# Expert rows fetched from and added to HBM by indirect transfers in a mixture-of-experts decoder trunk

## The reference

```python
def swiglu(h, w_gate_up, w_down):
    g, u = jnp.split(h @ w_gate_up, 2, axis=-1)
    return (jax.nn.silu(g) * u) @ w_down

def moe_ffn(h, router, w_gate_up, w_down):
    t = h.reshape(B * S, D)                       # 256 x 1024
    logits = (t @ router).astype(jnp.float32)     # 256 x 8
    top_v, top_i = lax.top_k(logits, TOP_K)
    gates = jax.nn.softmax(top_v, axis=-1)
    combine = jnp.sum(jax.nn.one_hot(top_i, N_EXPERTS) * gates[..., None], axis=1)
    out = jnp.zeros_like(t)
    for e in range(N_EXPERTS):                    # w_gate_up[e]: 1024 x 7168, w_down[e]: 3584 x 1024
        out = out + combine[:, e:e + 1] * swiglu(t, w_gate_up[e], w_down[e])
    return out
```

## Time and profile before

| | us |
|---|---|
| median of 3 runs | 1529.01 (1528.96 to 1530.62) |
| the profiled execution, its own time | 1530.43 |
| its span in the profile | 1528.6 |
| PE busy | 1487.6 (97%) |
| DVE busy | 1166.1 (76%) |
| ACT busy | 963.4 (63%) |
| POOL busy | 32.6 (2%) |
| bytes moved | 431.78 MB, 282 GB/s over the span |

### The profile page before, as it was taken

One profiled execution on the slowest core, in us unless ns is written; L12 is line 12 of the kernel. 1 busy time (PEld: TensorE's weight loads), 2 busy tenths in 40 slices (PEclk: granted clock), 3 DMA queues, 4 the chain that ended last, 5 costly groups with the idle time before them and its releaser, 6 DMA issues.

```text
span 1528.6 us, 20344 instructions
## 1 busy us (share of the span) xinstructions
PE 1487.6 (97%) x7137; PEld 1251.9 (82%) x7137; DVE 1166.1 (76%) x914; ACT 963.4 (63%) x838; POOL 32.6 (2%) x81
## 2 busy tenths in 40 slices
PE   7999999999989899999999999999999999999997
PEld 7997788888878778888888888888888888888885
DVE  4566545554674599899899899889989989989985
ACT  6454544444683387777677677677767667767764
POOL 1010000000020000000000000000000000000000
PEclk9999999999999899999999999999999999999999
DMA  8544455554353389999999999999999999999992
GB/s 284 192 138 143 160 185 185 181 191 158 91 190 111 110 326 381 329 377 363 339 363 366 337 356 380 357 328 377 358 323 378 368 335 363 360 342 359 380 354 83
DMA packets 207522, 431.78 MB, mean 282 GB/s; under 512 B 14261, under 2 KB 54650, under 8 KB 207482
## 3 DMA queue, kind: packets, MB, share of 16 engines
q1 hardware_dynamic: 207194, 430.20, 78.9%
q0 software_dynamic: 288, 1.05, 0.2%
HBM read 430.15 MB, written 1.05 MB: 282 GB/s over the span
## 4 chain that ended last, share of the span: by engine, by line
PE 95%; DVE 2%; ACT 2%; issue 1%; SPq 0%; DMA 0%; ACTq 0%; DVEq 0%
PE PS L1530 19%; PE PS L1534 19%; PE PS L1531 19%; PE PS L1241 5%; PE PS L1242 5%; PE PS L1243 5%; PE PS L1005 4%; PE PS L1490 2%; PE PS L1055 2%; PE PS L1050 2%; PE PS L1052 2%; PE PS L1501 1%; PE PS L1104 1%; PE PS L1107 1%; PE PS L1101 1%
## 5 line engine op out<-in xcount | busy, mean ns | idle before, releaser
L1681 DVE TENSOR_TENSOR wlo<-ring,whi 128x2048 fp32r<-128x2048 f32 x334 | 762.7, 2291 | 114.0 <-ACT whi L662 112.3
L662 ACT ACTIVATE whi<-ring 128x2048 fp32r<-128x2048 f32 x334 | 639.6, 1918 | 233.2 <-PE PS L1534 222.1
L1530 PE MATMUL PS<-whi,xhi 128*128 128x512 f32 x864 | 341.1, 395 | 0.4 <-ACT whi L662 0.4
L1531 PE MATMUL PS<-whi,xlo 128*128 128x512 f32 x864 | 336.8, 390 | 0.0
L1534 PE MATMUL PS<-wlo,xhi 128*128 128x512 f32 x864 | 231.4, 390 | 0.2 <-DVE wlo L1681 0.2
L1534 PEld LDWEIGHTS PS<-wlo,xhi 128*128 128x128 f32 x864 | 162.1, 188 | 34.7 <-DVE wlo L1681 0.6
L1530 PEld LDWEIGHTS PS<-whi,xhi 128*128 128x128 f32 x864 | 162.3, 188 | 33.2 <-ACT whi L662 0.7
L1531 PEld LDWEIGHTS PS<-whi,xlo 128*128 128x128 f32 x864 | 162.4, 188 | 32.5
L1530 PE MATMUL PS<-whi,hhi 128*128 128x512 f32 x440 | 172.7, 393 | 0.0
L1531 PE MATMUL PS<-whi,hlo 128*128 128x512 f32 x440 | 171.3, 389 | 0.0
L1647 DVE TENSOR_TENSOR wlo<-ring,whi 128x2048 fp32r<-128x2048 f32 x42 | 96.3, 2292 | 67.4 <-ACT whi L630 67.4
(11 more groups left out here) (333 smaller groups left out, 1650.4 us busy)
## 6 DMA issues: line engine op xcount, KB each, us to landing
ring<-in_moe_w_gate_up SPq DMA_DIRECT2D x448, 512.0 KB, 5.4
ring<-in_moe_w_down SPq DMA_DIRECT2D x224, 512.0 KB, 5.5
ring<-in_dense_w_gate_up SPq DMA_DIRECT2D x56, 512.0 KB, 4.6
ring<-in_dense_w_down SPq DMA_DIRECT2D x28, 512.0 KB, 4.2
ring<-in_a_w_in SPq DMA_DIRECT2D x12, 768.0 KB, 7.6
ring<-in_mem_w_kv SPq DMA_DIRECT2D x4, 1024.0 KB, 5.3
ring<-in_a_w_out SPq DMA_DIRECT2D x4, 1024.0 KB, 4.9
ring<-in_b_w_out SPq DMA_DIRECT2D x4, 1024.0 KB, 5.0
```

Source lines behind the costliest of these rows:

```text
L662: nc.scalar.activation(whi[:, j, :], ring[:, h * SLOT:(h + 1) * SLOT], ACT.Copy).then_inc(S("highs"), 1)
L1530: mm(out_, lhsT=xh, rhs=whi[:, j, c0:c0 + HD], start=first, stop=False)
L1531: mm(out_, lhsT=xl, rhs=whi[:, j, c0:c0 + HD], start=False, stop=False)
L1681: v.tensor_tensor(wlo[:, j, :], ring[:, h * SLOT:(h + 1) * SLOT], whi[:, j, :].bitcast(F32), ALU.subtract).then_inc(S("lows"), 1)
```

## The change

**Tokens to an expert.** The normalised tokens are stored once to a scratch tensor `xg` in HBM, and the residual stream once to the output itself. From expert 1 on, POOL fetches the rows of the next expert by an indirect transfer (`fetch_rows`) with a list of token numbers, one for each slot (`slot_tok`), into `xs` (the SBUF of `xn`), as rows. PE turns them with 8 transposes (`turn_rows`) at block 6. Expert 0 still uses `gather`.

**The list.** `slot_values` replaces `turn_gates`: two products of `Sx` with two columns `ct`, the gate and the token's number. It runs at block 3 and 5 of expert 0 and at block 5 of the others; DVE copies both columns. The keys are made otherwise: a token that isn't chosen gets a place behind the chosen ones, so that every one of the 256 keys of an expert is used and each of the 128 slots holds a different token, with gate 0 where the token wasn't chosen. That needs `counts` and more DVE steps.

**Results back.** In block 1 ACT writes gate times y as one f32 tile `ys` (`y_out`), and POOL adds its 128 rows to the output in HBM by an indirect transfer with addition (`put_rows`). `combine`, `y_low`, `G` and `add` are gone, and SP's final store too. After the last expert, ACT and DVE each do half of y, and POOL does the last `put_rows` and waits for all of them.

**Waits.** PE waits at block 6 for `rows_in` ahead of `turn_rows`. DVE waits at block 4 for the last scatter (`putting`, `scattered`) before it overwrites gate and list, and at block 5 for `slots_turned` and `fetching`. POOL's `pause` operations (one element each) order its transfers with DVE. Some semaphores are merged (`q_t` and `k_t` into `heads_t`, others alike), which changes no order; POOL's `iota` comes earlier.

```diff
+        xg_d = nc.dram_tensor("xg", [SEQ, D], F32)
+        xs, ys = xn[0:CAP, 0], xn[0:CAP, 1]
@@ sync
-            for t in range(NT):
-                sp.wait_ge(S("x_final"), t + 1)
-                sp.dma_start(out[0].rearrange("(t p) d -> p t d", p=P)[:, t], xres[:, t]).then_inc(S("stored"), 16)
-            sp.wait_ge(S("stored"), 16 * NT)
@@ gpsimd
+            pool.wait_ge(S("x_sum"), 9)
+            for t in range(NT):
+                pool.dma_start(out[0][t * P:(t + 1) * P], xres[:, t]).then_inc(S("stored"), 16)
+            pool.wait_ge(S("x3_gained"), 1)
+            for t in range(NT):
+                pool.dma_start(xg[t * P:(t + 1) * P], xn[:, t]).then_inc(S("xg_in"), 16)
+            pool.wait_ge(S("xg_in"), 16 * NT)
+            def fetch_rows(i):
+                pool.wait_ge(S("slots"), i + 1)
+                pool.tensor_tensor(pause, nhalf[0:1, 0:1], nhalf[0:1, 0:1], ALU.mult).then_inc(S("fetching"), 1)
+                pool.indirect_dma_start(xs, None, xg, bass.IndirectOffsetOnAxis(ap=slot_tok[:, 0:1], axis=0)).then_inc(S("rows_in"), 16)
+            def put_rows(n):
+                pool.wait_ge(S("y_out"), n)
+                pool.tensor_tensor(pause2, nhalf[0:1, 0:1], nhalf[0:1, 0:1], ALU.mult).then_inc(S("putting"), 1)
+                pool.indirect_dma_start(out[0], bass.IndirectOffsetOnAxis(ap=put_tok[:, 0:1], axis=0), ys, None,
+                                        compute_op=ALU.add).then_inc(S("scattered"), 16)
+            fetch_rows(0)
+            pool.wait_ge(S("stored"), 16 * NT)
+            with pool.Fori(1, passes * NE) as i:
+                put_rows(i)
+                fetch_rows(i)
+            pool.wait_ge(S("y_half"), 1)
+            put_rows(passes * NE)
+            pool.wait_ge(S("scattered"), passes * (NE * 16))
@@ scalar
-            def y_high():
-                nc.scalar.activation(yhi, PS[0:CAP, 4:6, :].rearrange("p a (k n) -> p (a k) n", n=P), ACT.Copy,
-                                     scale=gate[:, 0:1]).then_inc(S("y_high"), 1)
+            def y_out(cols):
+                nc.scalar.activation(ys[:, 0:cols], PS[0:CAP, 4:6, :].rearrange("p a n -> p (a n)")[:, 0:cols], ACT.Copy,
+                                     scale=gate[:, 0:1]).then_inc(S("y_out"), 1)
@@ tensor
-            def turn_gates():
+            def slot_values():
                 for t in range(NT):
-                    tr(PS[0:CAP, 2, t * P:(t + 1) * P], Sx[:, t, :])
-                for t in range(NT):
-                    last = mm(PS[0:CAP, 2, SEQ:SEQ + 1], lhsT=Sx[:, t, :], rhs=combe[:, t:t + 1], start=(t == 0), stop=(t == NT - 1))
-                last.then_inc(S("G_turned"), 1)
+                    last = mm(PS[0:CAP, 2, 0:2], lhsT=Sx[:, t, :], rhs=ct[:, t, :], start=(t == 0), stop=(t == NT - 1))
+                last.then_inc(S("slots_turned"), 1)
+            def turn_rows():
+                for k in range(KD):
+                    last = tr(PS[:, 6 + k // 4, (k % 4) * CAP:(k % 4 + 1) * CAP], xs[:, k * P:(k + 1) * P])
+                last.then_inc(S("gathered"), 1)
@@ tensor, expert
-                    if not first and b == 2:
-                        combine(0, 6, i)
-                    if not first and b == 3:
-                        pe.wait_ge(S("added0"), i)
-                        combine(1, 6, i)
-                    if b == 4:
-                        if first:
-                            pe.wait_ge(S("gates"), 1)
-                        turn_gates()
+                    if first and b == 3:
+                        pe.wait_ge(S("gates"), 1)
+                        pe.wait_ge(S("iota"), 2)
+                        slot_values()
                     if b == 5:
                         pe.wait_ge(S("dispatch"), i + 2)
-                        if not first:
-                            pe.wait_ge(S("added1"), i)
-                        gather()
+                        slot_values()
+                    if b == 6:
+                        pe.wait_ge(S("rows_in"), i * 16 + 16)
+                        turn_rows()
@@ vector, next_dispatch
-                dve.wait_ge(S("G_turned"), i + 1)
-                v.tensor_copy(G[:, :, :], PS[0:CAP, 2, 0:SEQ].rearrange("p (t s) -> p t s", t=NT)).then_inc(S("G_ready"), 1)
-                v.tensor_copy(gate, PS[0:CAP, 2, SEQ:SEQ + 1])
+                if is_first(i):
+                    dve.wait_ge(S("slots_turned"), 1)
+                    then(v.tensor_copy(gate_next, PS[0:CAP, 2, 0:1]))
+                    then(v.tensor_copy(slot_tok, PS[0:CAP, 2, 1:2]))
+                else:
+                    dve.wait_ge(S("putting"), i)
+                    dve.wait_ge(S("scattered"), i * 16)
+                then(v.tensor_copy(gate, gate_next))
+                then(v.tensor_copy(put_tok, slot_tok))
@@ vector, expert
-                    if b == 1 and not first:
-                        y_low(i)
-                    if b in (2, 3) and not first:
-                        add(i, f"added{b - 2}", b - 2, 6)
+                    if b == 5:
+                        if not first:
+                            dve.wait_ge(S("fetching"), i)
+                        dve.wait_ge(S("slots_turned"), i + 2)
+                        v.tensor_copy(gate_next, PS[0:CAP, 2, 0:1])
+                        v.tensor_copy(slot_tok, PS[0:CAP, 2, 1:2]).then_inc(S("slots"), 1)
@@ vector, keys of expert 0
-            dve.wait_ge(S("ranks"), 1)
-            then(v.scalar_tensor_tensor(out=keys[:, :, 0:NE], in0=PS[:, 3, 0:NT * NE].rearrange("p (t n) -> p t n", t=NT),
-                                        scalar=4096.0, in1=chosen, op0=ALU.add, op1=ALU.mult))
-            then(v.tensor_scalar(keys[:, :, 0:NE], keys[:, :, 0:NE], -4096.0, None, ALU.add))
+            dve.wait_ge(S("counts"), 1)
+            for t in range(NT):
+                last = v.tensor_scalar(oh2k[:, t], PS[:, 5, 0:NE], ct[:, t, 1:2], None, ALU.add)
+            then(last)
+            then(v.tensor_tensor(oh2k, oh2k, PS[:, 3, 0:NT * NE].rearrange("p (t n) -> p t n", t=NT), ALU.subtract))
+            then(v.tensor_tensor(first_keys, PS[:, 3, 0:NT * NE].rearrange("p (t n) -> p t n", t=NT), oh2k, ALU.subtract))
+            then(v.tensor_tensor(first_keys, first_keys, chosen, ALU.mult))
+            then(v.tensor_tensor(first_keys, first_keys, oh2k, ALU.add))
@@ vector, end
-            y_low(passes * NE)
-            for t, bank in enumerate((6, 0)):
-                add(passes * NE, "x_final", t, bank)
+            dve.wait_ge(S("through"), passes * (NE * PERE) + NS)
+            v.tensor_scalar(ys[:, HD:D], PS[0:CAP, 5, :], gate[:, 0:1], None, ALU.mult).then_inc(S("y_half"), 1)
```

More of the change, by code:

```diff
@@ L98, in build, with is_first @@
     assert PERE == PER and PERE % SLOTS == 0 and PERE % CUTS == 0
+    def is_first(i):
+        return isinstance(i, int) and i == 0
     def expert_item(i, b, q):
-        return 6 * b + q - (0 if b == 0 and isinstance(i, int) else 2)
+        return 6 * b + q - (0 if b == 0 and is_first(i) else 2)
     def expert_parts(gu, dn, b, q):
@@ L296, in build @@
         cnt_i = sb("cnt_i", [P, 1], I32)
-        G = sb("G", [CAP, NT, P], FR)
+        xg_d = nc.dram_tensor("xg", [SEQ, D], F32)
+        xg = xg_d.ap()
+        tok_i = arena[:, o:o + NT].bitcast(I32); o += NT
+        slot_tok = arena[:, o:o + 1].bitcast(I32)[0:CAP]; o += 1
+        pause = arena[0:1, o:o + 1]; o += 1
+        put_tok = arena[:, o:o + 1].bitcast(I32)[0:CAP]; o += 1
+        pause2 = arena[0:1, o:o + 1]; o += 1
+        xs, ys = xn[0:CAP, 0], xn[0:CAP, 1]
         NORMS = ["x0", "mem", "mq0", "mk0", "hm", "mk1", "x1", "x2", "ckv", "cq", "mq1", "kh", "qh", "x3a", "x3b"]
@@ L383, in upto @@
         def upto(i, per_expert, const):
-            return const if isinstance(i, int) else i * per_expert + const
+            return i * per_expert + const
         def cut_item(b):
@@ L487, in load_expert @@
                     for q in range(6):
-                        if isinstance(i, int) and b == 0 and q >= 4:
+                        if is_first(i) and b == 0 and q >= 4:
                             continue
@@ L585, in _ @@
             pool.tensor_copy(iota, iotai).then_inc(S("iota"), 1)
+            pool.iota(tok_i, pattern=[[P, NT]], base=0, channel_multiplier=1).then_inc(S("iota_i"), 1)
+            pool.wait_ge(S("iota_i"), 2)
+            pool.tensor_copy(ct[:, :, 1], tok_i).then_inc(S("iota"), 1)
+            rstd_of("x3a")
+            rstd_of("x3b")
+            pool.wait_ge(S("x_sum"), 9)
[14 more added lines that the diff above has]
+                                        compute_op=ALU.add).then_inc(S("scattered"), 16)
+            pool.wait_ge(S("routed"), 1)
+            passes = pool.value_load(cnt_i[0:1, 0:1], min_val=1, max_val=PASSES)
+            fetch_rows(0)
[6 more added lines that the diff above has]
+            pool.wait_ge(S("scattered"), passes * (NE * 16))
         @block.scalar
@@ L669, in expert @@
             def expert(i):
-                first = isinstance(i, int)
```

(18 more changed lines are left out.)

37 lines of the change are left out of this document (17 added, 20 removed).

## The result

The changed kernel takes 1495.88 us (median of 4 runs, 1492.31 to 1496.84) where the kernel before took 1529.61: a ratio of 0.9775, 95% interval 0.9757 to 0.9792. The forecast was 1494, range 1489 to 1515. Its profiled execution took 1492.31 us, with a span of 1490.5.

The account below looks back on a forecast made before the run. PE, busy without a gap, was taken to set the expert period of 123.83 us. Span 1528.6 - 36.1 (PE work) - 3.1 (end) + 1.5 (ahead of experts) + 2.4 (DMA) = 1493.3, time 1494 us, range 1489 to 1515.

Parts of the forecast that it names:

- PE's work: PE in the experts: 4.80 us less in each of experts 1 to 7, 2.5 in expert 0, together 36.1 us.
- ACT and DVE hidden: ACT and DVE in the experts: DVE's 109.46 us don't grow, idle time in 119.03 covers new waits; cost nothing.
- The rows: PE's wait for fetched rows at block 6: 14.9 us available, fetch bounded at 4.0 to 12.2; cost nothing.
- the price had they been late: Late rows at block 6: every microsecond beyond 14.9 costs PE eight; rival's chance 0.08.
- DMA: Expert traffic: 45.61 MB at 393 GB/s takes 116.1 us against PE's 119.03; DMA engines becoming the bound had chance 0.20.
- the term of 2.4 us: DMA in the experts: 0.3 us added per expert for dips so close to the limit, 2.4 us.
- Ahead of the experts: Between router and dispatch: keys wait for counts (0.74 us) and a longer DVE chain (0.75), 1.5 us more on the path.
- The end: After the last product: half y on ACT and DVE, 0.4 us pause, a 6 us scatter; 3.1 us less than 10.2.
- The sum: Whole kernel: span 1528.6 - 36.1 - 3.1 + 1.5 + 2.4 = 1493.3; time 1494 us, chance of 1490 to 1499 0.62.
- My two wrong terms, +2.4 and -3.1: Expert traffic near the DMA limit, 2.4 us more, and the stretch after the last product, 3.1 us less.

Follow-up runs that it names:

- light: Changed kernel with three quarters of every second transfer of the down weights left unloaded: 1496.25 us, beside 1494.12 for the changed kernel.
- heavy2: Changed kernel with two more POOL loads of 512 KB per expert into unused SBUF: 1497.11 us, beside 1494.12 for the changed kernel.
- pool_writes: Changed kernel with four POOL fills of 128x1024, which read nothing, behind every fetch: 1494.12 us.
- last_plain: Changed kernel whose last scatter overwrites its rows without adding: 7.2 us from ACT's half of y to the span's end at 1489.3, for 10.3.
- counts_first: Changed kernel with PE's counts ahead of the ranks and DVE waiting for ranks only after its two column steps: 1494.47 us.
- add_only: Changed kernel with the row fetch undone and the 16-product gather back, results still added in HBM: 1516.62 us, beside 1494.12.
- the second profile: Profiled execution of the changed kernel run again with nothing edited: span 1494.2 us, 3.7 more than the first; median of its runs 1494.12 us.
- late1: Changed kernel with POOL's fetch also waiting until PE has done the second cut of block 6: 1535.37 us, ratio 1.0034 to the kernel before.
- late3: Changed kernel with POOL's fetch also waiting until PE has done the fourth cut of block 6: 1578.98 us in one run.
- pool_reads: Changed kernel with four POOL products of 128x1024 with two SBUF operands behind every fetch: 1546.92 us.

## Why the prediction was right, point by point

- **PE's work** (36.1 us) was right in every term. turn_rows took 0.79 and the usual 0.09, 0.88 as estimated; slot_values 0.36 and 0.09. The period was forecast as 119.03 and is 119.0 to 119.1 in the profiles of the changed kernel (two), light, heavy2, pool_writes, last_plain and counts_first. add_only measures the two parts by themselves: 2.6 us of the period for the gather, forecast 2.70, and 2.16 for combine and turn_gates, forecast 2.10.
- **ACT and DVE hidden**: right. DVE 106.2 of 119.
- **The rows**: right. 14.9 us were forecast between list and turn; the gate_up ends of blocks 5 and 6 are 17.30 us apart for the forecast 17.25, and the rows land some 9.3 us after the list is ready (736.05 to 745.4), inside the bounds 4.0 to 12.2. Some 5.5 us are spare. What was wrong is the price had they been late: I left out the reduced clock behind a wait.
- **DMA**: the rate was right (392 for 393), the term of 2.4 us was not; it measured nothing, both by less traffic and by 2% more (387 GB/s). I had smeared a limit that is sharp over a range in which the ring absorbs it.
- **Ahead of the experts**: 1.5 forecast; chosen to Sx went from 1.89 (513.53 to 515.42 in the kernel before) to 3.45, so 1.56. What reached the path is another matter. Expert 0's first product starts only 0.92 us later (523.50 before, 524.42 in the second profile), because the gather in front of it ran at a higher granted clock (0.65 for 0.58). Then 1.1 us are lost again between the silu of blocks 1 and 2 of expert 0 (14.19 us before, 15.29 after), at 0.89 for 1.00 of the clock. At the silu of block 5 the changed kernel is 1.80 us behind (616.85 and 618.65), where my terms make 1.3.
- **The end**: the second error. 3.1 us less than 10.2 were forecast; it took 10.3 and 10.0 in the two profiles. The landing of 6.4 us was close to my 6, but from the two halves of y to the issue it takes 0.85 (1480.95 to 1481.80) where I had 0.4, and from landing to the end of the span 2.3, where the plain stores before had 0.5 (about 1525.5 + 2.6 to 1528.6) and I had nothing.
- **The sum**: from the silu of block 5 of expert 0 to ACT's reading of the last y the changed kernel is 36.0 us shorter (901.59 and 865.57), for 35.9 of my terms; ahead of it stand 1.8 us of loss, and 0.2 are won at the end: 34.4, as the two spans have it. My two wrong terms, +2.4 and -3.1, nearly cancelled, so 1494 was closer than its working deserved. That is luck.
- **Not foreseen**: the spread of the total. In code that the change doesn't touch, the first profile of the changed kernel is 3.2 us shorter than the other two, at a higher clock; taken alone with the one before, it would have given 38.1.

## What to carry to other kernels

Where one engine is busy without a gap, its removed instructions can be summed from start to start of the rows, and the sum holds until the next resource is reached; find that resource's full rate in a stretch where its queue is long, and, if the buffers are as deep as here (six slots of 1 MiB), treat it as a step. Indirect transfers from POOL are a good place for the ends of an expert as long as there are some 10 us between list and use, and the last one, which nothing hides, costs as much as the one-hot product did. A wait of PE can cost more than its length: behind the waits of 3.2 to 9.5 us here the matmuls ran slower for a while.

## What the runs showed of the hardware that I had not expected

- POOL's one-element operation and the fetch's descriptor generation last as if they waited for the end of a DVE subtraction that runs. The pause of 658.77 lasts 0.81 us, to 659.58, and DVE's subtraction of 657.24 ends at 659.53; without one it lasts 0.18. The fetch of 736.48 takes 2.93 us beside a subtraction that runs from 736.22 to 738.51; in late1, issued at 880.93, 0.23 us ahead of the next subtraction, it takes 1.01.
- A scatter of 128 rows of 4 KB with addition takes POOL 1.60 us, without 0.98, and moves its bytes at less than half the rate (3.8 us for 1.4).
- 3.5 us of idle time of PE are followed by some 2.3 us of extra time at a reduced clock (late1), 9.2 us by 2.1 (late3), 4.4 us by about 2.8 (pool_reads: period 126.2, 7.15 above 119.05), and 1.07 us by none (late1, last expert, granted clock 1.00 from 1508.3 to 1514 us).
